# Two-direction delta-rule scan: head sums on 32 rows, the second direction half a chunk behind, readout inside the scan

## What is computed

```python
def rwkv_features(h, mu, w_rkv, w0, w1, w2, a0, a1, a2, k_k, k_a):
    ...                              # r, k, v: 16 heads of 64; decay per direction
    kk = k * k_k
    kk = kk / jnp.maximum(jnp.sqrt(jnp.sum(kk * kk, axis=-1, keepdims=True)), 1e-12)
    k = k * (1.0 + (a - 1.0) * k_a)
    return r, k, v, -kk, kk * a, decay, xg

def step(s, inp):                    # wkv_scan, once forward, once in reverse
    sa = jnp.einsum('bhvk,bhk->bhv', s, a_t)
    s = s * w_t[:, :, None, :] + sa[..., None] * b_t[:, :, None, :] + v_t[..., None] * k_t[:, :, None, :]
    return s, jnp.einsum('bhvk,bhk->bhv', s, r_t)

def rwkv_readout(y_fwd, y_bwd, r, k, v, xg, g1, g2, r_k, gn_g, gn_b, w_o):
    bonus = jnp.sum(r * k * r_k, axis=-1, keepdims=True) * v
    gate = lambda d: jax.nn.sigmoid(xg @ g1[d]) @ g2[d]
    o = (group_norm(y_fwd, gn_g, gn_b) + bonus) * gate(0) + (group_norm(y_bwd, gn_g, gn_b) + bonus) * gate(1)
    return o @ w_o
```

## Time and profile before

| what | value |
|---|---|
| median of three runs | 3868.96 us |
| lowest and highest | 3861.84, 3869.44 us |
| the profiled execution: its time | 3871.23 us |
| its span | 3869.4 us |
| mean granted TensorE clock | 0.944 |
| TensorE busy | 3362.6 us, 87% |
| VectorE busy | 1243.5 us, 32% |
| ScalarE busy | 639.5 us, 17% |
| GpSimd busy | 206.8 us, 5% |

### The profile page before, as it was taken

How to read it: one execution, slowest core, us unless ns; L and a number is a source line. 1 busy time by engine, 2 the same in 40 slices (tenths; PEclk the granted TensorE clock), 3 DMA queues, 4 the chain that set the end, 5 groups by cost and what they waited for, 6 DMA issues and landing times.

```text
span 3869.4 us, 68275 instructions
## 1 busy us (share of the span) xinstructions
PE 3362.6 (87%) x29368; PEld 2366.8 (61%) x29368; DVE 1243.5 (32%) x2312; ACT 639.5 (17%) x1207; POOL 206.8 (5%) x185
## 2 busy tenths in 40 slices
PE   7997899998888899999889989999877876885899
PEld 5675465655767455655576644444367765884688
DVE  1335132333233323323255521100244436446210
ACT  0101111111110111111133310000023222231000
POOL 0000000000000000000000000000005401340000
PEclk9998999999898999999999989999898987997899
DMA  7646396998474479969604521222130021001342
GB/s 272 234 180 245 137 390 280 382 391 349 155 283 173 164 285 375 403 276 383 256 24 148 190 87 54 76 76 77 60 112 4 4 83 52 4 4 44 122 152 107
DMA packets 113816, 686.18 MB, mean 177 GB/s; under 512 B 11024, under 2 KB 11184, under 8 KB 49456
## 3 DMA queue, kind: packets, MB, share of 16 engines
q1 hardware_dynamic: 109920, 668.69, 45.0%
q0 software_dynamic: 3536, 12.17, 0.9%
HBM read 679.76 MB, written 1.05 MB: 176 GB/s over the span
## 4 chain that ended last, share of the span: by engine, by line
PE 40%; DVE 6%; issue 2%; ACT 2%; POOL 1%; DVEq 0%; ACTq 0%; POOLq 0%; PEldq 0%
PE ps L203 15%; PE ps L1427 9%; PE ps L1934 6%; PE ps L1748 4%; DVE arena L136 3%; ACT arena L119 2%; PE ps L533 1%; POOL arena L136 1%; PE ps L560 1%; DVE arena L156 1%; PE ps L1793 1%; PE ps L335 1%; DVE arena L140 1%; PE ps L548 1%; DVE arena L145 0%
## 5 line engine op out<-in xcount | busy, mean ns | idle before, releaser
L203 PE MATMUL ps<-arena 128*128 128x256 f32 (+1 forms) x3552 | 998.2, 444 | 100.3 <-DVE arena L136 31.4
L203 PEld LDWEIGHTS ps<-arena 128*128 128x128 f32 x3552 | 693.3, 196 | 398.8 <-issue 258.2
L119 ACT ACTIVATE arena<-ps 128x512 f32<-128x512 f32 (+1 forms) x524 | 264.2, 504 | 1550.0 <-PE ps L203 698.8
L1080 PE MATMUL ps<-arena 128*64 128x256 f32 x4096 | 487.6, 388 | 36.9 <-DVE arena L145 23.8
L1080 PEld LDWEIGHTS ps<-arena 128*64 128x64 f32 x4096 | 318.2, 140 | 204.1 <-issue 63.6
L1427 PE MATMUL ps<-arena 128*128 128x512 f32 (+1 forms) x1024 | 330.6, 486 | 0.0
L1934 PE MATMUL ps<-arena 64*64 64x64 f32 x10496 | 285.3, 220 | 30.3 <-issue 27.3
L136 DVE TENSOR_TENSOR arena<-arena,ps 128x512 f32<-128x512 f32 (+1 forms) x272 | 160.2, 589 | 440.6 <-PE ps L1934 223.1
L1934 PEld LDWEIGHTS ps<-arena 64*64 64x64 f32 x10496 | 279.2, 136 | 35.9 <-issue 31.1
L1427 PEld LDWEIGHTS ps<-arena 128*128 128x128 f32 x1024 | 194.6, 190 | 135.7 <-issue 122.5
L136 DVE TENSOR_TENSOR arena<-arena 128x256 f32<-128x256 f32 (+6 forms) x250 | 168.8, 675 | 328.1 <-ACT arena L119 318.1
(11 more groups left out here) (167 smaller groups left out, 2436.8 us busy)
## 6 DMA issues: line engine op xcount, KB each, us to landing
arena<-in_w_gate SPq DMA_DIRECT2D x128, 1024.0 KB, 8.2
arena<-in_w_up SPq DMA_DIRECT2D x128, 1024.0 KB, 11.8
arena<-in_w_down SPq DMA_DIRECT2D x128, 1024.0 KB, 8.7
arena<-in_mlp SPq DMA_DIRECT2D x64, 1024.0 KB, 4.7
arena<-in_w_ada SPq DMA_DIRECT2D x48, 1024.0 KB, 7.0
arena<-in_ada SPq DMA_DIRECT2D x48, 1024.0 KB, 4.8
arena<-in_w_in SPq DMA_DIRECT2D x30, 1024.0 KB, 5.8
arena<-in_w_rkv SPq DMA_DIRECT2D x20, 1024.0 KB, 4.7
```

The costliest lines, as they stand in the source:

```text
L119: self.e.activation(out, in_, func, bias=bias, scale=scale, **more).then_inc(*self.done(key))
L203: ins = pe.matmul(out, a, b, start=start and i == 0, stop=stop and i == len(pairs) - 1)
L1080: ins = pe.matmul(psum.of["gu", l, new][64 * ab:64 * ab + 64, i_ * 256:i_ * 256 + 256], xe[:, k, new % 2 * 128 + 64 * ab:new % 2 * 128 + 6 ...
```

## The change

- **TensorE's waits**: all go through `reach`, which leaves a wait out where TensorE has already waited for that semaphore at that value or a higher one. At a branch (`over`) the record is set back to what held before it.
- **Head sums on 32 rows**: `head_sum` multiplies by a 128x32 matrix, so that four column blocks land on the four groups of 32 partitions of one bank, and all 16 heads' sums fit in 128x512. Root, maximum and reciprocal work on 128x512, and `spread_pe` with `spread_dve` bring the result back to all rows. It is used for the kk norm of both s and for the variance of both directions; mean and bonus keep `sums_pe`. The two constant matrices are loaded over `tri`.
- **Features**: `kd` (k times k_a) and k times (1 - k_a) are formed while the root is awaited; the last three products are done in two halves. For s = 0 the gates of both directions are made here, and ScalarE copies them into the ring's tiles 3 and 4; the ring is cut to three tiles for the loads of g1, g2 and w_o.
- **Scan**: `in_turn` gives the first direction eight steps ahead of the second, for both s.
- **Readout**: the bonus is formed inside the scan of s = 0 (r times k on VectorE in chunk 1, eight ScalarE operations at chunk 1 level 3 and eight at chunk 2 level 3, the sums and products at chunk 2). `read_pe`, `read_act` and `read_dve` are chained behind each direction's scan as three more steps, so that direction 0 is read out between the last steps of direction 1. The gain, the bonus and the bias are added in one operation per column block.

```diff
+        def reach(pe, sem, n):
+            if reached.get(sem, 0) < n:
+                pe.wait_ge(sem, n)
+                reached[sem] = n
...
-            sums_pe(pe, ("kk", s), R.xx, ("kk squared", s))
+            reach(pe, *at["scan"])
+            reach(pe, *at["kk squared", s])
+            b, old = psum.take(("kk sums", s), ("kk root", s))
+            freed(pe, old)
+            for k in range(8):
+                ins = head_sum(pe, b, k, R.xx)
+            ins.then_inc(*made(("kk sums", s)))
             wide(2, bufs[(n + 2) % 2], range(2, 4))
+            spread_pe(pe, ("kk", s), R.rows, ("kk inverse", s))
             lora("a", bufs[(n + 3) % 2], 4, 64, R.low[1], 1)
+            if s == 0:
+                for d in range(2):
+                    w = weights.of["g1", d][:, 0:1024].rearrange("p (k c) -> p k c", k=8)
...
+                    group(pe, b[:, 0:256], [(w[:, k, :], R.xg[:, k, :]) for k in range(8)]).then_inc(*made(("gate low", d)))
...
+        def head_sum(pe, b, k, src):
+            j = 32 * (k % 4)
+            return pe.matmul(b[j:j + 32, k // 4 * 256:k // 4 * 256 + 256], tri[:, 0:32], src[:, k, :], start=True, stop=True)
+
+        def spread_pe(pe, key, rows, ready):
+            reach(pe, *at[ready])
...
+            for h in range(2):
+                for j in range(4):
+                    ins = pe.matmul(psum.of[key, "spread", j][:, h * 256:h * 256 + 256], tri[32 * j:32 * j + 32, 32:160],
+                                    rows[32 * j:32 * j + 32, h * 256:h * 256 + 256], start=True, stop=True)
...
-            dve.wait_ge(*at[("kk", s), "out", 3])
-            do.ts(xx, xx, 1e-12, None, ALU.max, None)
-            do.rcp(xx, xx)
-            do.tt(R.kk, R.kk, xx, ALU.mult)
-            dve.wait_ge(*at["up a out", s, 0, 7])
-            do.tt(R.b, R.kk, R.aT, ALU.mult)
             for k in range(8):
-                do.ts(R.aT[:, k, :], R.aT[:, k, :], vec("k_a")[:, k:k + 1], R.kvec[:, k:k + 1], ALU.mult, ALU.add)
-            do.tt(R.k, R.k, R.aT, ALU.mult)
+                do.ts(R.kd[:, k, :], R.k[:, k, :], vec("k_a")[:, k:k + 1], None, ALU.mult, None)
+            for k in range(8):
+                do.ts(R.k[:, k, :], R.k[:, k, :], R.kvec[:, k:k + 1], None, ALU.mult, None)
+            dve.wait_ge(*at["kk root", s])
+            do.ts(R.rows, R.rows, 1e-12, None, ALU.max, None)
+            do.rcp(R.rows, R.rows, ("kk inverse", s))
+            spread_dve(dve, do, ("kk", s), R.kk)
...
-        def in_turn(*ways):
-            ways = list(ways)
+        def in_turn(first, second):
+            for _ in range(8):
+                next(first)
+            ways = [first, second]
...
+                if (s, d, j) == (0, 0, 2):
+                    sums_pe(pe, "bonus", R.bonus, "bonus part")
...
+                    if (s, d, j, lev) == (0, 0, 1, 3):
+                        act.wait_ge(*at["rk"])
+                        for k in range(8):
+                            do.act(R.bonus[:, k, :], R.bonus[:, k, :], ACT.Copy, "bonus part" if k == 7 else None,
+                                   scale=vec("r_k")[:, k:k + 1])
...
+        def read_pe(pe, d):
+            sums_pe(pe, ("mean", d), R.Y[d], ("y out", 0, d, chunks(d)[-1]))
+            yield
...
+            for k in range(8):
+                if k % 2 == 0:
+                    reach(pe, *at["square", d, k // 2])
+                ins = head_sum(pe, b, k, R.tq[d])
+            ins.then_inc(*made(("var sums", d)))
+            yield
+            spread_pe(pe, ("var", d), R.var[d], ("var inverse", d))
+            yield
...
+        def read_dve(dve, d):
...
+            dve.wait_ge(*at["var root", d])
+            do.rcp(R.var[d], R.var[d], ("var inverse", d))
+            yield
+            spread_dve(dve, do, ("var", d), Yd)
+            dve.wait_ge(*at["bonus done"])
+            for k in range(8):
+                do.stt(Yd[:, k, :], Yd[:, k, :], vec("gn_g")[:, k:k + 1], R.bonus[:, k, :], ALU.mult, ALU.add)
+            dve.wait_ge(*at["gate up out", d, 3])
+            do.tt(Yd, Yd, R.G[d], ALU.mult, ("gate used", d))
...
-                in_turn(scan_pe(pe, s, 0), scan_pe(pe, s, 1))
+                in_turn(*(chain(scan_pe(pe, s, d), read_pe(pe, d) if s == 0 else ()) for d in range(2)))
```

More of the change, by code:

```diff
@@ L1 @@
 import math
+from itertools import chain
 from contextlib import ExitStack
@@ L1785, in sums_pe, with spread_dve @@
+        def spread_dve(dve, do, key, dst, done=None):
+            for j in range(4):
+                dve.wait_ge(*at[key, "spread", j])
+                do.tt(dst[:, j:8:4, :], dst[:, j:8:4, :], psum.of[key, "spread", j][:, :].rearrange("p (c t) -> p c t", c=2),
+                      ALU.mult, (key, "spread out", j))
         def sums_pe(pe, key, src, ready):
-            pe.wait_ge(*at["scan"])
-            pe.wait_ge(*at[ready])
+            reach(pe, *at["scan"])
+            reach(pe, *at[ready])
@@ L2132, in scan_dve @@
                               bc(m.mG[:, 0:ne, :], 1, n), ALU.mult, key(name + " out", q))
+                if (s, d, j) == (0, 0, 1):
+                    dve.wait_ge(*at["gate low", 1])
+                    do.tt(R.bonus, R.r, R.k, ALU.mult, "rk")
+                if (s, d, j) == (0, 0, 2):
+                    for q in range(4):
+                        dve.wait_ge(*at["bonus", q])
+                        do.tt(R.bonus[:, 2 * q:2 * q + 2, :], R.vT[:, 2 * q:2 * q + 2, :],
+                              psum.of["bonus", q][:, :].rearrange("p (c t) -> p c t", c=2), ALU.mult, ("bonus", "out", q))
                 yield
@@ L2202, in rwkv_sp @@
                 load(sp, ("rw_o", i), ("read out", 2 * i + 1), D["rw_o"][i])
+            weights.size = NRING
+            for d in range(2):
+                weights.used[3 + d] = [("gate used", d)]
         def rwkv_pe(pe, pump):
@@ L2235, in rwkv_pe @@
                     freed(pe, old)
-                    group(pe, b[:, 0:256], [(w[:, k, c * 128:c * 128 + 128], R.Oh[:, k, :]) for k in range(8)]) \
-                        .then_inc(*made(("read out", 2 * i + c)))
+                    for k in range(8):
+                        if i == c == 0 and k % 2 == 0:
+                            reach(pe, *at["both", k // 2])
+                        ins = pe.matmul(b[:, 0:256], w[:, k, c * 128:c * 128 + 128], R.Y[0][:, k, :], start=k == 0, stop=k == 7)
+                    ins.then_inc(*made(("read out", 2 * i + c)))
             end("read out", "pe", made)
```

309 lines of the change are left out of this document (160 added, 149 removed).

## The result

The changed kernel takes **3810.05 us**, median of 4 runs from 3807.15 to 3814.93. The kernel before, run beside it, takes 3869.2 (3861.84 to 3872.05, 4 runs). The ratio is 0.9851, 95% interval 0.9834 to 0.9868: 59 us faster, where 41 were forecast. 3810 lies in the range of 3800 to 3856.

The account below looks back on a forecast made before the run. Scans were taken as bound by instructions (3.6 us per 256) nearly as much as by TensorE, the readout by VectorE. Terms -5.4 + 4 + 2 + 22 - 64 = -41 us took 3869 to 3828, range 3800 to 3856.

Parts of the forecast that it names:

- Waits left out ... I take 0: TensorE's matmul groups beginning with waits fall from 2168 to 1622; forecast effect 0 us, array fed ahead.
- The bound of 8 us from 14 ns of instruction supply: If each of the 546 waits took an instruction place at 14 ns, leaving them out would be -8 us.
- The fourth rival: A group's first weight load waits behind a spent wait, 8 us or more: 3820 us or below, chance 0.03.
- The falsifier in the text: Prediction would be wrong if, among other signs, the first 2777 us moved by more than 8.
- Features, -5.4 and +4: Feature stages: s = 1 -5.4 us (-2 to -8); s = 0 +4 us (0 to +9), gates moved in.
- The tail that sticks out behind the gates: Features of s = 0: gates add 14.5 us on TensorE, VectorE tail covers most, some 9 us sticks out.
- Scan of s = 1, +2: Scan of s = 1: 204 us, +2 (-10 to +12), with lone phases and blocks at 3.6 us between.
- The rival of TensorE's own pace: Both scans: blocks come evenly, pauses vanish, 3.27 and 3.40 us a block; 24 us less, 3804, chance 0.12.
- the lag buys no density: Scans' middle stays at 3.9 us a block, reading direction 0 beside direction 1 delays both; 3855 us, chance 0.12.
- Scan of s = 0, +22: Scan to direction 1's last output: 256 against 233 us, +22 (+8 to +35), including 38 us for its last steps.
- Behind the scan, -64: Readout before the projection: one direction left, 26 us instead of 90.1, -64 (-68 to -58).
- The low clock: Behind the scan: 2 us allowed for TensorE's low clock, on top of 24 us of steps.

## Why the prediction was right, and where it was wrong

The direction, the mechanism of the large terms and the range held. The total was 18 us short by the runs, and two terms that failed partly cancel. That 3810 lies in the range owes something to luck: had the second scan cost what I gave it, the time would have been near 3798, just below the range.

- **"Waits left out ... I take 0"** is the step that failed. It measured -24.7 us alone. The argument looked at the scan, where 30 groups run without a gap; there it may hold. But the 546 groups stand in all stages, and some 20 us lie in the experts, from which I read no row. The bound of 8 us from 14 ns of instruction supply was the wrong bound. It counted groups, while most of what goes out of the instruction stream are semaphore instructions of their own: TensorE executes 744 fewer (1465 before, 721 after), which at 14 ns would still be only 10 us. Another mechanism can be larger, and nothing in the trace had excluded it. The fourth rival, "waits matter more than I see ... 8 us or more: 3820 or below", is what came, and had 0.03. The falsifier in the text, the first 2777 us moving by over 8, caught it. Spread over the 579 fewer semaphore instructions ahead of the mixer it would be 43 ns each, an average and no price of one, since 278 of them lie outside the experts and brought some 4 us.
- **Features, -5.4 and +4**: measured -4.3 and +3.7. The tail that sticks out behind the gates was the right reading: TensorE has 12.7 us more busy time in s = 0, the stretch is only 3.7 longer.
- **Scan of s = 1, +2**: +3.9, inside the spread of equal kernels. The lone phases cost more (27.1 where I had 21), and the middle ran at 3.77 us a block, not 3.6. The rival of TensorE's own pace (3.27 a block, no pauses) falls with this: the pauses after 128 records are in mid-chunk now. What makes them stays open, since no run isolates the fetch. Of the rival "the lag buys no density" the first half holds: 3.77 lies nearer to today's 3.9 than to 3.6, and taking the lag out changes nothing.
- **Scan of s = 0, +22** (256 against 233 is +23 as the terms stand): +34. The tail is right (38 forecast, 36.3 measured). Of the 12 missing, 7 are the bonus (18.3 against 11.6), where I counted ScalarE in front of a copy and not VectorE's 128x2048 product in front of the levels; 5 are direction 1's later start.
- **Behind the scan, -64**: -67.5, the operations near what was named. The low clock is in the stretch (0.66), and its 2 us were right in sign.
- **By the runs**, all but the waits is -35.9 with the sum at -41: the terms that I worked out promised 5 us too much, and the one I waved through brought 25.

What stays open: which of the spent waits in the experts cost, why a wait that is met costs at all, and what sets the 3.8 us per 256 instructions. Not tried was leaving the waits out in the other halves of the expert loop alone.

## What to carry to other kernels

A wait that is already satisfied isn't free to a TensorE queue just because no gap stands behind it in one stage: before it is priced at nothing, look at every stage that holds one, or leave it out, since it costs nothing to do. A shift of two interleaved chains fills the holes at their common starts and pays at its two ends; where the middle is held by something else (here 3.8 us per 256 instructions), it comes to nothing. For work put into "idle" slots of in-order queues count every engine that it uses: the bonus cost 18 us where I had 12. And put it there in single operations: sixteen one by one instead of eight in a row brought 14 us without the lag and 5 with it. A count of blocks or instructions that follows from the program is no evidence of what bounds it.

## What the runs showed that I had not expected

- 1860 spent conditions (746 semaphore instructions) left out of TensorE's queue give 24.7 us of 3869 (ratio 0.9939, 0.9923 to 0.9954); 1161 of them, all outside the expert stages, give 4 (0.9978 to 1.0003).
- Two profiles of all but the same instructions ahead of the mixer took 2777.6 and 2764.4 us; a difference of that size in one profile needs runs beside it.
- Semaphore increments stand 0.15 us apart in TensorE's queue, 2048 of them in an MLP added 210 us to the kernel, and a scan full of them runs at a mean granted clock of 0.57 instead of 0.96.
- A product of 128x2048 in fp32 took VectorE 2.29 us by itself and 3.14 while GpSimd ran its own 128x512 products beside it.
- Sixteen matmul records on 32 columns or 32 rows of the array took 1.07 and 1.15 us, where 16 on all 128x128 took 3.72.
